# A two-part transformer stack on one core: orders changed in the scan, in the even block, in the odd block and at both ends of the expert stages

## The reference

```python
# even layer: a state space scan, chunk by chunk, and a convolution branch
s_final, s_in = lax.scan(_carry_step, s0, (chunk_decay, chunk_states))
y_diag = einsum("bclsg,bclsgr,bcsgrp->bclgrp", cb, decay, xdt)
y_off  = einsum("bclgn,bcgrpn,bclgr->bclgrp", cc, s_in, exp(acum))
o_cf   = silu(layernorm(dwconv(v * sigmoid(gate))))
y      = concatenate([o_ssd, o_cf]) @ w_out
# odd layer: the same kind of scan with a decay for each key channel
o = o_intra + o_inter;  y = (rmsnorm(o) * silu(g)) @ w_out
# experts: each token goes to 2 of 16
y = (silu(t @ wg) * (t @ wu)) @ wd;  out += gate * y
```

## Time and profile before

| | |
|---|---|
| median of 3 runs (lowest, highest) | 2366.4 us (2358.8, 2370.4) |
| profiled execution, its own time | 2367.2 us |
| its span | 2365.5 us |
| busy: PE, DVE, ACT, POOL | 90%, 71%, 58%, 12% |
| mean granted TensorE clock | 0.951 of 2.4 GHz |
| HBM read and written | 432 MB and 21 MB, 191 GB/s over the span |
| scan, from the first sums to the last gate | 1072 to 1188 us |
| even block's products | 1194 to 1312 us |
| expert stages with what follows | 1338 to 1692 us, 2019 to 2358 us |
| odd block | 1694 to 2006 us |

### The profile page before, as it was taken

How to read it: one execution, slowest core, us unless ns; L and a number is a source line. 1 busy time by engine, 2 the same in 40 slices (tenths; PEclk the granted TensorE clock), 3 DMA queues, 4 the chain that set the end, 5 groups by cost and what they waited for, 6 DMA issues and landing times. The chain is left out here.

```text
span 2365.5 us, 36221 instructions
## 1 busy us (share of the span) xinstructions
PE 2135.6 (90%) x12334; PEld 1752.8 (74%) x12334; DVE 1684.0 (71%) x2810; ACT 1377.5 (58%) x2158; POOL 277.8 (12%) x357
## 2 busy tenths in 40 slices
PE   4999999989998999988899799999599998799995
PEld 4899876679997566666767477787488887577784
DVE  4885544558746488988775589998537765699995
ACT  2664414446536245666553478887458863588884
POOL 0000000000000056556500001110100000011100
PEclk8999999999999999998999899999799998899998
DMA  6455341265542666630012299999332222699993
GB/s 220 162 185 172 130 146 51 71 250 188 170 156 99 236 234 225 232 132 1 1 54 89 107 363 387 388 387 388 113 101 78 72 76 77 233 397 392 397 396 138
DMA packets 127303, 454.97 MB, mean 192 GB/s; under 512 B 13873, under 2 KB 17841, under 8 KB 127025
## 3 DMA queue, kind: packets, MB, share of 16 engines
q1 hardware_dynamic: 116208, 413.14, 47.7%
q0 software_dynamic: 10944, 39.85, 4.6%
HBM read 431.97 MB, written 20.97 MB: 191 GB/s over the span
## 5 line engine op out<-in xcount | busy, mean ns | idle before, releaser
L2793 DVE TENSOR_TENSOR moe_w_lo<-ring,moe_w_hi 128x1024 fp32r<-128x1024 f32 x384 | 462.8, 1221 | 57.6 <-ACT moe_w_hi L2728 52.5
L2728 ACT CAST moe_w_hi<-ring 128x1024 fp32r<-128x1024 f32 x384 | 399.0, 1049 | 124.1 <-PE ps L236 116.6
L373 DVE TENSOR_TENSOR ffn_w_lo<-ring,ffn_w_hi 128x1024 fp32r<-128x1024 f32 x132 | 161.0, 1222 | 101.2 <-ACT ffn_w_hi L325 101.1
L234 PE MATMUL ps<-moe_w_hi,moe_own 128*128 128x512 f32 x480 | 198.4, 413 | 6.8 <-DVE moe_hid L2806 6.0
L325 ACT CAST ffn_w_hi<-ring 128x1024 fp32r<-128x1024 f32 x132 | 137.4, 1044 | 107.5 <-PE ps L236 107.5
L236 PE MATMUL ps<-moe_w_hi,moe_own 128*128 128x512 f32 x480 | 190.6, 397 | 0.0
L235 PE MATMUL ps<-moe_w_lo,moe_own 128*128 128x512 f32 x480 | 190.5, 397 | 0.0
L234 PE MATMUL ps<-ffn_h_hi,ffn_w_hi 128*128 128x256 f32 x608 | 173.3, 285 | 11.2 <-DVE ffn_w_lo L373 11.2
L235 PE MATMUL ps<-ffn_h_lo,ffn_w_hi 128*128 128x256 f32 x608 | 172.0, 283 | 0.0
L236 PE MATMUL ps<-ffn_h_hi,ffn_w_lo 128*128 128x256 f32 x608 | 172.0, 283 | 0.0
L234 PE MATMUL ps<-ffn_hid,ffn_w_hi 128*128 128x256 f32 x448 | 130.9, 292 | 13.6 <-DVE ffn_w_lo L373 9.7
(11 more groups left out here) (579 smaller groups left out, 5690.0 us busy)
## 6 DMA issues: line engine op xcount, KB each, us to landing
ring<-in_weights SPq DMA_DIRECT2D x766, 512.0 KB, 5.3
expert_rows<-moe_y POOLq DMA_DIRECT2D x32, 512.0 KB, 7.0
token_rows<-moe_token_rows SPq DMA_DIRECT2D x6, 512.0 KB, 3.4
sq<-in_cmp_w SPq DMA_DIRECT2D x1, 2048.0 KB, 8.1
both<-in_x SPq DMA_DIRECT2D x1, 1024.0 KB, 5.8
both<-in_context SPq DMA_DIRECT2D x1, 1024.0 KB, 8.0
out<-both SPq DMA_DIRECT2D x4, 256.0 KB, 2.2
cols<-in_cols SPq DMA_DIRECT2D x1, 720.5 KB, 9.0
```

The lines of the kernel that those rows point to most:

```text
L234: pe.matmul(out, w_hi, x_hi, start=start, stop=False)
L373: dve.tensor_tensor(w_lo[:, u % WB], k.ring[:, (first + u) % RING], w_hi[:, u % WB], ALU.subtract).then_inc(w_split, 1)
L2728: act.copy(w_hi[:, j % WB].rearrange("p h f -> p (h f)"), k.slot(act, first + GU + j, e).rearrange("p a f -> p (a f)")).then_inc(w_rounded, 1)
L2793: dve.tensor_tensor(w_lo[:, j % WB].rearrange("p h f -> p (h f)"), k.ring[:, (first + GU + j) % RING].rearrange("p a f -> p (a f)"), w_hi[ ...
```

## The change: what it does

1. In the scan GpSimd's loop does `fade(u)` first, then `weigh`, then `take_tap`.
2. In the even block ACT drains and casts after every second Silu and splits one half slot after each pair; VectorE's scalings, splits, products and low parts are interleaved to match.
3. The first expert's gate and up sums go to the banks `DOWN` and `DOWN + 1`; in turn 0 TensorE no longer waits for `hidden` before the sums, and turns `hid` behind the third slot. A one-column Silu stands ahead of ACT's first rounding of the rows.
4. The last expert's rows are stored by a DMA that ACT issues, with a semaphore of its own, `y_last`, for which GpSimd waits at the end of the stage.
5. In the odd block the first `keep_turned(0, 0)` moves from the start of round 2 to the end of round 1, ahead of `logs_of(1)`; in round 8 ACT takes the tiles of `places[0]` before `exps(7, 1)`.

```diff
 # ssd, gpsimd
                 for u in range(NU):
+                    if 2 * SG <= u < NU - 2 * SG:
+                        fade(u)
                     if u % SG == 0 and u // SG + 1 < NU // SG:
                         weigh(u // SG + 1)
                     take_tap(EARLY + u)
-                    if 2 * SG <= u < NU - 2 * SG:
-                        fade(u)
 # even_out, scalar
                     act.activation(cf[:, t, :], cf[:, t, :], ACT.Silu, scale=ln_g[:, t:t + 1], bias=ln_b[:, t:t + 1])
-                    act.drain()
-                    act.copy(cf_hi[:, t, :], cf[:, t, :]).then_inc(c_rounded, 1)
-                    if t % 4 == 3:
-                        next_splits(4 + t // 4)
+                    if t % 2:
+                        act.drain()
+                        for own in (t - 1, t):
+                            act.copy(cf_hi[:, own, :], cf[:, own, :]).then_inc(c_rounded, 1)
+                        split(2 * 4 + WB + t // 2)
 # even_out, vector
-                for t in range(KD):
-                    dve.tensor_tensor(cf[:, t, :], cf[:, t, :], c_root, ALU.mult).then_inc(c_normed, 1)
-                    if t % 4 == 3:
-                        next_splits(4 + t // 4)
-                        take_product(4 + t // 4)
-                for t in range(KD):
-                    dve.wait_ge(c_rounded, t + 1)
-                    dve.tensor_tensor(cf_lo[:, t, :], cf[:, t, :], cf_hi[:, t, :], ALU.subtract).then_inc(c_split, 1)
-                for n in range(6, NS):
+                scale_c(0, 4)
+                split(2 * 4 + WB)
+                scale_c(4, 6)
+                split(2 * 4 + WB + 1)
+                take_product(4)
+                scale_c(6, KD)
+                split(2 * 5 + WB)
+                low_c(0, 4)
+                split(2 * 5 + WB + 1)
+                take_product(5)
+                low_c(4, 6)
+                split(2 * 6 + WB)
+                low_c(6, KD)
+                split(2 * 6 + WB + 1)
+                take_product(6)
+                for n in range(7, NS):
                     next_splits(n)
                     take_product(n)
 # moe_experts, gpsimd
                     if e >= 0:
-                        pool.wait_ge(y_taken, e + 1)
-                        pool.dma_start(y_hbm[e * P:(e + 1) * P, :], y[:, :]).then_inc(y_stored, 16)
-                pool.wait_ge(y_stored, 16 * EXPERTS)
+                        if e < EXPERTS - 1:
+                            pool.wait_ge(y_taken, e + 1)
+                            pool.dma_start(y_hbm[e * P:(e + 1) * P, :], y[:, :]).then_inc(y_stored, 16)
+                pool.wait_ge(y_last, 16)
 # moe_experts, tensor
-                        if down:
+                        if down and (looped or e > 0):
                             pe.wait_ge(hidden, e + 1)
-                            slot(e, at + t, (of[:, 0, t, :], of[:, 1, t, :]), UP, t == 0, t == GU - 1)
+                            slot(e, at + t, (of[:, 0, t, :], of[:, 1, t, :]), UP if down else DOWN, t == 0, t == GU - 1)
-                            if t == 0 and down:
+                            if t == (0 if looped or e > 0 else 2) and down:
                                 turn_hid(e)
 # moe_experts, scalar (gate and, in the same way, hide on vector read DOWN for the first expert)
-                    act.activation(act_g[:, :], k.ps[:, UP, :], ACT.Silu).then_inc(gated, 1)
+                    act.activation(act_g[:, :], k.ps[:, DOWN if isinstance(e, int) and e < 0 else UP, :], ACT.Silu).then_inc(gated, 1)
                 split(-1, 4, 5, 6, 7)
+                act.activation(act_g[:, 0:1], k.ones[:, 0:1], ACT.Silu)
                 rounds(act, turn)
+                act.wait_ge(y_taken, EXPERTS)
+                act.dma_start(y_hbm[(EXPERTS - 1) * P:EXPERTS * P, :], y[:, :]).then_inc(y_last, 16)
 # odd_mixer, scalar
-                        if live(h - 2):
+                        if live(h - 2) and h > 2:
                             keep_turned(h - 2, 0)
                         if live(h - 2):
                             keep_turned(h - 2, 1)
+                        if h == GH:
+                            for n in places[0]:
+                                take(n)
                         if live(h - 1):
                             exps(h - 1, 1)
-                        for n in places[0]:
-                            take(n)
+                        if h != GH:
+                            for n in places[0]:
+                                take(n)
+                        if h == 1:
+                            keep_turned(0, 0)
                         if live(h):
                             logs_of(h)
```

More of the change, by code:

```diff
@@ L2386, in _, with scale_c, low_c @@
                 take_product(3)
-                for t in range(KD):
-                    dve.tensor_tensor(cf[:, t, :], cf[:, t, :], c_root, ALU.mult).then_inc(c_normed, 1)
-                    if t % 4 == 3:
-                        next_splits(4 + t // 4)
-                        take_product(4 + t // 4)
-                for t in range(KD):
-                    dve.wait_ge(c_rounded, t + 1)
-                    dve.tensor_tensor(cf_lo[:, t, :], cf[:, t, :], cf_hi[:, t, :], ALU.subtract).then_inc(c_split, 1)
-                for n in range(6, NS):
+                def scale_c(first, last):
+                    for t in range(first, last):
+                        dve.tensor_tensor(cf[:, t, :], cf[:, t, :], c_root, ALU.mult).then_inc(c_normed, 1)
+                def low_c(first, last):
+                    for t in range(first, last):
+                        dve.wait_ge(c_rounded, t + 1)
+                        dve.tensor_tensor(cf_lo[:, t, :], cf[:, t, :], cf_hi[:, t, :], ALU.subtract).then_inc(c_split, 1)
+                scale_c(0, 4)
[14 more added lines that the diff above has]
+                for n in range(7, NS):
                     next_splits(n)
@@ L2805, in hide @@
                     dve.wait_ge(gated, e + 1)
-                    dve.tensor_tensor(hid[:, :], act_g[:, :], k.ps[:, UP + 1, :], ALU.mult).then_inc(hidden, 1)
+                    dve.tensor_tensor(hid[:, :], act_g[:, :], k.ps[:, (DOWN if isinstance(e, int) and e == 0 else UP) + 1, :], ALU.mult
+                                      ).then_inc(hidden, 1)
                 def pick_rows():
```

4 lines of the change are left out of this document (2 added, 2 removed).

## The result

The changed kernel takes 2322.5 us (median of 4 runs, 2322.2 to 2327.0) against 2366.3 us (median of 4, 2358.8 to 2370.4): a ratio of 0.9823, 95% interval 0.9807 to 0.9839. The forecast was 2325. A second set of runs of both kernels gave 0.9820 (0.9801 to 0.9839); one execution of the kernel before, of 10661 us, counts as slow and stands in no median or ratio here.

A forecast was written before the change was run, and what follows sets the result against it. TensorE, busy 90% of the span, was taken to lose time by standing still and running at half clock at the changed places; eight terms sum to 41.0 us, 2367.2 to 2326.2, median 2325 us, range 2312 to 2342.

The forecast's parts named there:

- Scan, 11 us: Scan units 9 to 24: fading first gains 15.7 us at most, less 4.9, so 11 us; range 6 to 15.7.
- late fade: Scan, second unit of each group: its fade stands behind product and tap, so VectorE waits 0.5 us.
- blocked calls: Scan: VectorE's product of two SBUF operands slows beside GpSimd's product, another 0.8 us in a group.
- Even block, 7.4: Even block, casts in pairs: 9.3 us can go, 1.9 given back for late halves; 7.4 us, range 5 to 9.3.
- First expert, 4.2 and 4.4: First expert's sums in DOWN end the wait for `hid`: 4.2 us first stage, 4.4 second; each 3 to 4.7.
- Last rows, 4.0 and 0.6: Store by ACT's queue: 4.0 us (1 to 6.5) in the first expert stage, 0.6 (0 to 1.5) in the last.
- Odd block, 4.6 and 4.8: Earlier copy of turned keys gains 4.6 us in round 2 (3 to 6); earlier Silus 4.8 in round 8 (2 to 5.2).
- (1): Scan's wait only moves to the second unit, gain there 5 us, even block and store low; 2336 us; chance 0.15.
- (2): Expert stages: the stream of weights is the bound, 8.6 us of head start given back; 2334 us; chance 0.12.
- (3): Scan: TensorE does not return to full clock; 2383 us with 24 units at half clock; chance 0.04.
- (4): Scan: product and VectorE each stand for the other's whole call, 1.9 us a group, 7.1 in all; 2327 us; chance 0.10.
- (5): The orders do not matter because other waits end at the same time; 2366 us; chance 0.03.

The follow-up runs named there:

- experts_mix: Changed kernel; first stage: old banks UP, early table load, GpSimd storing last rows before its gathers; second: new banks, no early load, SP storing; one run, 2330.9 us.
- part_one: Kernel before with the changes of the scan, of the first expert's banks (and early table load) and of round 2; 2340.5 us, ratio 0.9898.
- scan_tap_first: Changed kernel with GpSimd's scan order as fade, tap, product (product last); 2326.2 us, ratio 0.9833; units 9 to 24 took 53.0 us.
- part_two: Kernel before with the changes of the even block, the store and round 8; 2346.4 us, ratio 0.9913.
- scan_small_product: Changed kernel with GpSimd's large scan product cut from 64 to 2 columns of each head from the third on; one run, 2320.2 us.
- even_vector_only: Changed kernel with ScalarE's even-block order as before and VectorE's new order; one run, 2332.5 us; even block 57.8 us.

## Why the prediction was right

The sum of 41.0 us against 43.7 was right, and so were nearly all of its terms; the forecast erred by 2.5 us, less than single runs of one kernel differ by. (The low ends as added give 2343 us, the range says 2342.) The waits that were to go are gone, each at its place. Some of the closeness is luck: the scan's term, the largest, is measured against an old order that took 62.8 to 65.5 us in three traces, so it could have come out at 10.8 or at 13.5.

- **Scan, 11 us**: measured 12.1 (means) and 11.8 (first pair). The base was right: the pace without product is 48.2 us for 15 units. What is left over it was put down to a late fade (0.5 us a group) and to blocked calls (0.8), 4.9 us in all; it is 3.8 us. The blocked tap of VectorE (0.74 us) is as large as said. The late fade of the second unit is there in every group, a sign that the prediction had listed for being wrong, but it is small (0.2 to 0.5 us, 1.4 us in four groups; the terms as written, 2.22 + 1.36 + 1.22 + 0.2, give 5.0 and not 5.3 us, so 0.3 us). The step that was missing is ScalarE: it can scale the next tap only when GpSimd has added the last one, so it stands 2.1 us in each group (8.4 us in four; 2.4 us in three before), and VectorE then waits about 0.7 us for its exponentials. I had followed what GpSimd's product delays on VectorE, and not on ScalarE. That the rest came near 4.9 us without it is luck.
- **Why the old order was dear**: I said that the waits "cost more than that", by the half clock. The rows show this to be the greater part: 7.5 of 12.0 us.
- **Even block, 7.4**: 8.0. I gave 1.9 us back for late halves, of which the three that I named add up to 1.7; TensorE waits 0.27 us twice. The two engines' orders that I had followed together are needed together, as the two runs show.
- **First expert, 4.2 and 4.4**: 4.7 and 4.4; the mean of the first stage holds one trace of before that is 1.5 us longer than the other (45.7 us), against the first it is 4.1. TensorE waits 0.17 us for the first low part. The prediction gave the table load no term of its own, and `experts_mix` shows that it is worth nothing.
- **Last rows, 4.0 and 0.6**: 4.9 and 0.8 (0.6 or nothing, like with like), the first from 2.6 to 7.4 between single pairs of traces. I had two ends, landing as slowly as before or at once, and took a value between them; that the mean fell there is in part luck. The Trainium skill, "DMA: Bandwidth & Descriptors", section "SWDGE vs HWDGE vs iDMA", says that each DMA engine takes the two kinds of queue in turn. The prediction's estimate from that rule was about 5 us to landing; 3.1 to 6.2 were measured in ten traces.
- **Odd block, 4.6 and 4.8**: 4.7 and 4.1. TensorE's next wait in round 2 is VectorE's mask, 1.59 us at 1753.87, as worked out (1779.5 + 1.6 + 5.45 is 1786.6 and not 1786.7, which changes nothing, since the mask comes later). Round 8 brought 2.8 us between `part_one` and the changed kernel and up to 5.4 between others. In `part_one` TensorE waits the same 2.92 us as in the earlier trace rows, and the products after it take 0.28 us and not 0.41:

```profile
1905.89 0.36 PE L234 MATMUL ps<-hg_h_hi,hg_w_hi 128*128 128x256 f32 x1 [2.92 <-ACT both L3341]
...
1906.32 0.28 PE L234 MATMUL ps<-hg_h_hi,hg_w_hi 128*128 128x256 f32 x1
```

The part above 2.9 us is the half clock, which does not always follow. The prediction took it as given.

- **Rivals.** (1), the wait moves to the second unit: only 1.4 us in four groups. (2), the weights are the bound: 30.2 us of lead stayed 30.2. (3), half clock in the scan: the clock is 1.00. Its price was misread: of the two slow units only the first step was 5.62 us, the second 4.65. (4), the block of whole calls: it is real, 2.23 us for 0.69 in `scan_tap_first`, but in the changed order the product costs 1.0 us a group with all that follows and not 1.9; even with the product last it costs 4.8 us in all, 1.3 a group. (5), other waits end at the same time: those left at these places are 1.6 us or less.
- Of the 44.7 us between the first two spans 43.2 lie in the eight stretches. Ahead of the scan 5.0 us are gained; 2.5 us are lost between the odd block's last stretch of the table and the second expert stage, and 2.7 us in that stage's last turn. In all three places executions with the same work differ as much.

## What to carry to other kernels

Price a stall by the rows that follow it. Look whether the next products run at the full or at the half clock: in the scan the half clock made 7.5 of the 12.0 us, and in round 8 the same wait of 2.92 us cost nothing more in one trace and 2.6 us more in another. When an engine's long call is moved, ask for all engines that its later work feeds (here ScalarE's scaling, behind a tap), and try it in pieces: four quarters cost 0.4 us where the whole cost 3.8. Where two engines hand a buffer on, reorder both; one alone brought 1.3 or 3.6 us of 8.3. And before a gain of a few microseconds is booked, take several traces of the same kernel: here the first unit of the scan alone moved by 5 us.

## What the hardware showed that was not expected

One and the same wait of TensorE does not always cost the same. In the last turn of the second expert stage it stands 2.82 us for the turned hidden rows in every kernel; the products after it, kernel before, then changed kernel:

```profile
2330.35 0.50 PE L234 MATMUL ps<-moe_w_hi,moe_hid_t 128*128 128x512 f32 x1 [2.82 <-DVE moe_hid_t L2848]
...
2331.15 0.40 PE L234 MATMUL ps<-moe_w_hi,moe_hid_t 128*128 128x512 f32 x1
```
```profile
2284.01 0.79 PE L234 MATMUL ps<-moe_w_hi,moe_hid_t 128*128 128x512 f32 x1 [2.82 <-DVE moe_hid_t L2870]
...
2285.45 0.63 PE L234 MATMUL ps<-moe_w_hi,moe_hid_t 128*128 128x512 f32 x1
```

In the fourteen traces of this case the wait is 2.82 us each time. The clock was at its half level with the first product after it in eight (both of the changed kernel among them), fell a few products later in two (the second trace of before, `part_two`), and stayed full in four (the first of before, `scan_tap_first`, `scan_small_product`, `even_vector_only`). From the wait to the last product it takes 8.6, 7.4 and 5.9 us, so the half clock costs 0 to 2.7 us (the changed kernel's lead shrinks from 46.3 to 43.6 us there). The edits of the change do not lie near, and variants that share all work of this stage show both. What decides it stays open; the traces tell only that it is not the length of this wait alone. The four at full clock are also the four with the longer distance from copy to gather at the stage's end (5.2 to 5.4 us), so 0.6 to 1.2 us of what the clock saves is given back there.
